# Gated delta rule on one Trainium2 core: shared solve tiles, compact state, and a new order of outputs and scores

## The reference

```python
lower = where(tri_strict, einsum(k_beta, k) * decay, 0)
sol = triangular_solve(I + lower, [v_beta, k_beta * exp(g)])       # u, w
attn_intra = einsum(q, k) * decay
def step(state, inp):
    v_new = u_i - w_i @ state
    o_i = q_i @ state + a_i @ v_new                    # q_i carries exp(g)
    state = state * gl + k_i^T @ v_new                 # k_i carries exp(g_last - g)
```

## Time and profile before

| what | value |
|---|---|
| median of 3 runs (lowest, highest) | 2690.39 us (2690.27, 2694.24) |
| span of the profiled execution | 2685.3 us |
| busy, PE / PEld / DVE / ACT / POOL | 96% / 77% / 68% / 34% / 20% |
| mean granted TensorE clock | 0.985 |
| the changed loop | from about 397 to 603 us |

### The profile page before, as it was taken

The page is one execution under the profiler, slowest core; times in us unless marked ns, Lnnn a source line. Parts: engine busy times, 40 slices in busy tenths (PEclk is TensorE's granted clock), DMA queues, the critical chain, the costliest instruction groups (busy, mean ns, idle before and its releaser), DMA issues. The chain is left out here.

```text
span 2685.3 us, 35832 instructions
## 1 busy us (share of the span) xinstructions
PE 2583.9 (96%) x14026; PEld 2060.8 (77%) x14026; DVE 1817.1 (68%) x2735; ACT 926.3 (34%) x1610; POOL 549.2 (20%) x265
## 2 busy tenths in 40 slices
PE   7999999999899999999999999999999999999998
PEld 5875558884478887788888888867997888887787
DVE  5894997772667668999773553333277666666987
ACT  4335454420444545333332222232233223232432
POOL 1212544430000004333201222134400000003330
PEclk9999999999999999999999999999999999999999
DMA  4011032230133336333221222243413222225231
GB/s 162 32 64 67 32 126 96 90 133 24 55 114 118 103 118 223 111 110 126 91 82 53 78 70 75 81 166 108 145 55 88 79 87 79 87 79 214 100 126 63
DMA packets 192759, 262.24 MB, mean 98 GB/s; under 512 B 15952, under 2 KB 121808, under 8 KB 192208
## 3 DMA queue, kind: packets, MB, share of 16 engines
q1 hardware_dynamic: 192592, 259.95, 28.6%
HBM read 196.80 MB, written 61.93 MB: 96 GB/s over the span
## 5 line engine op out<-in xcount | busy, mean ns | idle before, releaser
L1381 PE MATMUL ps<-gl_t,gl_slot 128*128 128x512 f32 x1056 | 244.6, 391 | 2.4 <-DVE gl_t L3986 2.4
L1389 PE MATMUL ps<-b_hi,a_hi 128*128 128x512 f32 x592 | 231.6, 391 | 9.5 <-DVE sb L3630 7.6
L1381 PEld LDWEIGHTS ps<-gl_t,gl_slot 128*128 128x128 f32 x1056 | 199.3, 189 | 44.6 <-DVE gl_t L3986 3.1
L2756 POOL TENSOR_TENSOR s_raw<-ff_raw 128x1024 f32<-128x1024 f32 x2 | 5.1, 2545 | 962.6 <-DMA ff_raw<-hid_rows 513.6
L3630 DVE TENSOR_TENSOR sb<-sb,ps 128x512 f32<-128x512 f32 x272 | 173.5, 680 | 33.3 <-PE ps L1389 33.2
L1381 PE MATMUL ps<-gl_b,gl_slot 128*128 128x512 f32 x768 | 182.1, 395 | 3.7 <-DVE gl_slot L4018 3.7
L1381 PE MATMUL ps<-ff_t,slot 128*128 128x512 f32 x768 | 179.2, 393 | 4.4 <-DVE ff_t L3284 4.4
L1381 PE MATMUL ps<-H_hi,tw_hi 128*128 128x512 f32 x448 | 175.6, 392 | 0.0
L1381 PE MATMUL ps<-H_rest,tw_hi 128*128 128x512 f32 x448 | 174.4, 389 | 0.0
L1381 PE MATMUL ps<-H_hi,tw_lo 128*128 128x512 f32 x448 | 174.3, 389 | 0.0
L1381 PEld LDWEIGHTS ps<-gl_b,gl_slot 128*128 128x128 f32 x768 | 146.4, 191 | 35.1 <-DVE gl_slot L4018 2.4
(11 more groups left out here) (475 smaller groups left out, 6053.9 us busy)
## 6 DMA issues: line engine op xcount, KB each, us to landing
wraw<-in_w_ff SPq DMA_DIRECT2D x16, 1024.0 KB, 5.9
ff_raw<-ff_rows SPq DMA_DIRECT2D x8, 2048.0 KB, 7.9
slab_raw<-in_w_ff SPq DMA_DIRECT2D x16, 1024.0 KB, 5.1
ff_rows<-quad SPq DMA_DIRECT2D x61, 256.0 KB, 2.0
traw<-in_w_in SPq DMA_DIRECT2D x28, 512.0 KB, 4.3
wq_raw<-in_w_in SPq DMA_DIRECT2D x6, 2048.0 KB, 8.5
wraw<-in_w_gate SPq DMA_DIRECT2D x22, 512.0 KB, 3.9
wraw<-in_w_up SPq DMA_DIRECT2D x22, 512.0 KB, 5.1
```

The lines of the kernel that those rows point to most:

```text
L1381: mm = nc.tensor.matmul(out_ap, stationary(a, k), moving(c, k), start=(k == 0 and n == 0), stop=(k == kts - 1 and n == 2))
L1389: mm = nc.tensor.matmul(out_ap, stationary(a, k), moving(c, k), start=(fresh and k == 0 and n == 0), stop=(k == 1 and n == 2), skip_group_ ...
L2756: G.tensor_tensor(s1, s3, a22, ALU.add).then_inc(dn_as, 1)
```

## The change

Each line is what the code does.

- The values and the rest of the solve share tiles: `X_of(i, c)` is in `KVt[i % 2][c]`. Tile 0 holds direction 0's rows 0 to 63 and direction 1's rows 64 to 127, the halves both solve first; tile 1 holds the others. `kv_load` fills them with six transfers a step instead of two. `Xw` and its first copies on GpSimd are gone.
- One `forward` and one `less_forward` of 128 rows serve both directions. Forwards 1 and 2 write 64 rows a direction from 128; forward 3 writes 32 from 32. Heads alternate between the directions.
- The state `Sc` is compact (4x64 columns a direction, no zero blocks, no memset). `update` and `carried` go head by head.
- The decay on the carried keys is multiplied into `KdT` by GpSimd ahead, instead of scaling the product by `ECUM` on VectorE; `less_carried` is one subtraction per tile and half.
- "kk" and "kq" become one matmul of 256 columns a head ("sc"), in four parts a step, two a direction. The weights share a tile (`weights`), and GpSimd's `decay_args` waits for all four of a direction.
- Order: direction 0's outputs of the step before and its scores stay between the stages; the last own output of direction 1 and both parts of its scores stand behind the update, ahead of the carried term.
- The loads of `w_out` are cut: the first half's rows 0 to 3 wait for the last solve, and the residual's second half for the outputs of step 6.

```diff
-        Gm = [[area(AT_X + 4096 + 2048 * b + 1024 * d, HEADS, P) for d in range(2)] for b in range(2)]
-        ATm = [[area(AT_H + 2048 * b + 1024 * d, HEADS, P) for d in range(2)] for b in range(2)]
+        weights = [[area(at_g + 2048 * d, HEADS, 2, P) for d in range(2)] for at_g in (AT_X + 4096, AT_H)]
+        KQ = area(AT_WORK + 12288, 2, 4 * SEQ).rearrange("p n (q c) -> p n q c", c=SEQ)
         KVt = [[area(AT_W + 2048 * b + 1024 * d, 2 * GW) for d in range(2)] for b in range(2)]
+        KV_LOADS = 16 * 6
+        def X_of(i, c):
+            return KVt[i % 2][c][:, GW:2 * GW]
-        Xw = [area(AT_W + 6144 + 512 * d, GW) for d in range(2)]
-        Sbd = [[area(gd + 1024 * b + 512 * d, 4, P) for d in range(2)] for b in range(2)]
+        Sc = [[area(gd + 512 * b + 256 * d, 4, HD) for d in range(2)] for b in range(2)]
+        KdT = [area(gd + 1024 + 512 * d, 4, P) for d in range(2)]
...
+        def mixed_rows_of(i, c):
+            return tile_of(c, i), tile_of(1 - c, i)
...
             def kv_load(i):
                 if i >= 2:
-                    sp.wait_ge(gdn_X, 2 * (i - 1))
+                    solved(sp, i - 2)
                     sp.wait_ge(gdn_kd, 2 * (i - 1))
-                for d in range(2):
-                    sp.dma_start(KVt[i % 2][d], kv_rows[tile_of(d, i)]).then_inc(kv_in[i % 2], 16)
+                for c in range(2):
+                    dst = KVt[i % 2][c]
+                    sp.dma_start(dst[:, 0:GW], kv_rows[tile_of(c, i)][:, 0:GW]).then_inc(kv_in[i % 2], 16)
+                    for x, t in enumerate(mixed_rows_of(i, c)):
+                        part = slice(HD * x, HD * x + HD)
+                        sp.dma_start(dst[part, GW:2 * GW], kv_rows[t][part, GW:2 * GW]).then_inc(kv_in[i % 2], 16)
...
+            solved(sp, NT - 2)
+            wov_0, wov_1 = (w_out[:, 512 * h:512 * h + 512].rearrange("(k p) n -> p k n", p=P) for h in range(2))
+            sp.dma_start(wout_late, wov_0[:, 4:8]).then_inc(slab_in[0], 16)
+            sp.dma_start(wout_1, wov_1).then_inc(slab_in[1], 16)
             sp.wait_ge(gdn_rexp, 2 * NT)
             sp.wait_ge(gdn_arg, 2 * NT)
             for h in range(2):
                 if h == 1:
-                    for d in range(2):
-                        wait_full(sp, G_GDN, GDN_AT[("w", NT - 1, d, 3)])
+                    for p in range(4):
+                        wait_full(sp, G_GDN, GDN_AT[("o", NT - 2, p)])
                 sp.dma_start(X[:, 4 * h:4 * h + 4, :], xv[:, 4 * h:4 * h + 4, :]).then_inc(xin_in, 16)
+            solved(sp, NT - 1)
+            sp.dma_start(wout_early, wov_0[:, 0:4]).then_inc(wout_in, 16)
...
+            def scores(i, d, part):
+                if i >= NT:
+                    return
+                banks = [bank("sc", i, d, part, x) for x in both]
+                t = tile_of(d, i)
+                for j in both:
+                    for x in both:
+                        q = 2 * part + j
+                        keys_and_queries = KQ[HD * x:HD * x + HD, :, q, t * P:(t + 1) * P]
+                        mm = nc.tensor.matmul(heads_of(ps[:, banks[x], 256 * j:256 * j + 256], P), tokens(KTall, 2 * q + x, d, i),
+                                              keys_and_queries, start=True, stop=True)
+                        if j == 1:
+                            mm.then_inc(full[banks[x]], 1)
...
+            def carried(i, c):
+                for d in both:
+                    ready("kv", i - 1, d)
+                    pe.wait_ge(gdn_keys, 2 * (i - 1) + d + 1)
+                banks = [bank("kS", i, c, x) for x in both]
                 for q in range(4):
-                    mm = nc.tensor.matmul(ps[:, b, q * P:(q + 1) * P], pair_tile(KTall, q, d, i), Sbd[d][i % 2][:, q, :],
-                                          start=True, stop=True)
-                mm.then_inc(full[b], 1)
+                    for x in both:
+                        for r in both:
+                            d = c if r == 0 else 1 - c
+                            part = slice(HD * r, HD * r + HD)
+                            mm = nc.tensor.matmul(ps[part, banks[x], q * HD:(q + 1) * HD], half(KdT[d], 2 * q + x)[:, part],
+                                                  half(Sc[d][i % 2], 2 * q + x), start=True, stop=True)
+                        if q == 3:
+                            mm.then_inc(full[banks[x]], 1)
...
+            def forward(i, s):
+                for d in both:
+                    if s == 1:
+                        weights_ready(pe, i, d)
+                    ready("y", i, d, s - 1)
+                b = bank("w", i, s)
                 for h in range(HEADS):
-                    mm = nc.tensor.matmul(ps[rows, b, h * HD:(h + 1) * HD], Gm[i % 2][d][:, h, rows],
-                                          yv[i % 2][d][:, h * HD:(h + 1) * HD], start=True, stop=True)
+                    for d in both:
+                        rows = block_rows(d, 3) if s == 3 else slice(HD, P) if (s == 2) != (d == 1) else slice(0, HD)
+                        seen = block_rows(d, 2) if s == 3 else slice(0, P)
+                        mm = nc.tensor.matmul(ps[rows, b, h * HD:(h + 1) * HD], weights[i % 2][d][seen, h, 0, rows],
+                                              yv[i % 2][d][seen, h * HD:(h + 1) * HD], start=True, stop=True)
                 mm.then_inc(full[b], 1)
             def update(i, d):
@@ -1625,73 +1689,86 @@
                 ready("y", i, d, 3)
                 b = bank("kv", i, d)
                 for q in range(4):
-                    cols = slice(q * P, (q + 1) * P)
-                    mm = nc.tensor.matmul(ps[:, b, cols], Kdec[d][:, cols], yv[i % 2][d][:, cols], start=True, stop=True)
+                    for x in both:
+                        cols = slice((2 * q + x) * HD, (2 * q + x + 1) * HD)
+                        mm = nc.tensor.matmul(ps[x * HD:(x + 1) * HD, b, q * HD:(q + 1) * HD], Kdec[d][:, cols],
+                                              yv[i % 2][d][:, cols], start=True, stop=True)
                 mm.then_inc(full[b], 1)
-            def outputs(i, *parts):
-                for p in parts if i >= 0 else ():
-                    d = p // 2
-                    pe.wait_ge(gdn_qd, 2 * i + d + 1)
-                    ready("y", i, d, 3)
-                    for x in range(2):
-                        ready("kq", i, d, x)
-                    b = bank("o", i, p)
-                    for q in (2 * (p % 2), 2 * (p % 2) + 1):
-                        if i > 0:
-                            nc.tensor.matmul(ps[:, b, q * P:(q + 1) * P], QdT[(i + 2) % 3][d][:, q, :], Sbd[d][i % 2][:, q, :],
-                                             start=True, stop=False)
-                        for h in (2 * q, 2 * q + 1):
-                            cols = slice(h * HD, (h + 1) * HD)
-                            mm = nc.tensor.matmul(ps[:, b, cols], ATm[i % 2][d][:, h, :], yv[i % 2][d][:, cols],
-                                                  start=(i == 0), stop=(i == 0 or h % 2 == 1))
-                    mm.then_inc(full[b], 1)
...
             for i in range(NT):
                 more = i + 1 < NT
                 if i > 0:
-                    for d in both:
-                        carried(i, d)
-                outputs(i - 1, 0, 1)
+                    for c in both:
+                        carried(i, c)
                 solve(i, 0)
                 if i == 0:
                     for d in both:
-                        scores("kq", 0, d)
-                outputs(i - 1, 2)
-                for d in both:
-                    forward(i, d, 1)
-                outputs(i - 1, 3)
+                        first_scores("kq", d)
+                else:
+                    carried_outputs(i - 1, 0)
+                forward(i, 1)
+                if i > 0:
+                    own_outputs(i - 1, 0, 0)
                 solve(i, 1)
-                if more:
-                    scores("kk", i + 1, 0)
-                for d in both:
-                    forward(i, d, 2)
-                if more:
-                    scores("kq", i + 1, 0)
+                if i > 0:
+                    own_outputs(i - 1, 0, 1)
+                forward(i, 2)
+                scores(i + 1, 0, 0)
                 solve(i, 2)
-                if more:
-                    scores("kk", i + 1, 1)
-                for d in both:
-                    forward(i, d, 3)
-                if more:
-                    scores("kq", i + 1, 1)
+                scores(i + 1, 0, 1)
+                if not more:
+                    carried_outputs(i, 0)
+                forward(i, 3)
+                if i > 0:
+                    carried_outputs(i - 1, 1)
+                    own_outputs(i - 1, 1, 0)
                 solve(i, 3)
                 if more:
                     for d in both:
                         update(i, d)
-            outputs(NT - 1, 0, 1, 2, 3)
+                if i > 0:
+                    own_outputs(i - 1, 1, 1)
```

(149 more changed lines are left out.)

133 lines of the change are left out of this document (61 added, 72 removed).

## The result

The changed kernel takes 2751.86 us (2749.97 to 2753.36, 4 runs) against 2690.33 before: a ratio of 1.0227, interval 1.0213 to 1.0242. The forecast was 2694 with a range to 2712.

A forecast was written before the change was run, and what follows sets the result against it. It took a serial zigzag of four solves, beside a slower mask loop, to bound the loop. Terms -0.7 - 1.6 - 3.5 + 4.5 - 0.35 - 1.0 + 6.4 gave +3.7 us on 2690.39: 2694, range 2684 to 2712.

The forecast's parts named there:

- Shared tiles and one subtraction: Three forward stages of a step: one subtraction of 0.68 us, 0.72 less a stage; forwards one and two 1.1, third 1.08.
- The rival that column halves don't overlap: Forwards one and two and the update run longer: 2.5 us a step, 15 over six, 2709; chance 0.22.
- The prediction's sign against itself: First and second forward at 1.8 us or more for 32 records would show the forecast wrong.
- Update, carried term, moved work: Behind the last solve: update 1.1 us, own outputs 0.95, scores part 1.05, carried term 2.2; first solve starts at 6.8.
- The new wait: First copy stands behind ScalarE's exponentials: forward one 11.5 us behind the update, 2.3 longer; TensorE idle 2.6 us.
- The stall of the state's decay: VectorE's decay of the state beside GpSimd's four multiplications: 0.45 us a step charged, between 0 and 1.5.
- The clock: TensorE's new wait comes six times; four followed by half clock at 1.6 us: +6.4, between 0 and 18.
- six gaps at 3: Upper bound of the clock term: all six new waits of TensorE cost 3 us each, 18 us.
- Sum: All terms over loop start, steps, last step, tail and clock: +3.7 us on 2690.39, prediction 2694.
- clock falls at every gap and stays: Rival for TensorE's clock at the new waits: 6 x 3 = 18 us instead of 6.4, 2706; chance 0.14.

The follow-up runs named there:

- a6_apart: a1_copy_first with the forward's two loops exchanged, so one direction's records come first instead of alternating; 2706.48 us, ratio 1.0061.
- a2_fill: Changed kernel, wait kept, with two idle products of 128x512 ahead of forward one of steps 1 to 6, inside the wait; 2688.87 us, ratio 1.0008.
- a7_dense_later: Changed kernel, wait kept unfilled, with two idle products of 128x512 ahead of forward three of steps 1 to 6; 2745.11 us, ratio 1.0207.
- a1_copy_first: Changed kernel with direction 1's exponentials moved behind the second copy of the next step on ScalarE, instead of ahead of its first; 2692.93 us, ratio 1.0021.

## Why the prediction was wrong, point by point

**Shared tiles and one subtraction: right.** One subtraction of 0.68 to 0.69 a stage; forwards 1.15 (taken as 1.1) and third forward 1.08. The rival that column halves don't overlap fell: a6_apart shows it as an experiment. The Trainium skill, "TensorEngine Tiling (Array Packing)", section Tiling Modes, says that column tiles over all rows load and multiply independently; these runs agree where the records alternate (1.15 us) and not where they don't (1.87), which the trace of before could not show. The prediction's sign against itself, a forward of 1.8 us or more, would have misled: forward one does take 1.98 us, but by the clock, and 1.15 at full clock.

**Update, carried term, moved work: right within 0.2 us but for one term.** Update 1.15 (1.1), own outputs 1.10 (0.95), a part of the scores 1.00 (1.05), carried outputs 1.11 (1.0). The carried term was put at 2.2 us and took 1.20, since four blocks of 64x64 overlap; it changed nothing, as VectorE's weightings end last there.

**The new wait: right.** Forward one at 11.86 (11.5), idle 2.61 (2.6), once a step, released by ScalarE; in the steps behind this one the idle time is 3.15 to 3.31.

**The stall of the state's decay: right at full clock,** 0.40 to 1.35 us in a2_fill by where it meets GpSimd. In the changed kernel itself the two never meet, and it takes 0.40 to 0.42 each time.

**The clock: this step failed.** The text took four falls at 1.6 us, +6.4, between 0 and 18, with prices from two early waits of the old loop. The direction was right, and nearly the place: every one of steps 2 to 6 loses its clock at the wait. The size was off by ten: 2751.86 - 2688.87, with and without the filling, is 63 us. The failed term is the price of one fall. Steps 2 to 6 take 33.3 to 38.3 us, against 25.1 to 25.9 in a2_fill: 8 to 13 us a fall instead of 1.6, and no step is spared. The two prices had been read where half clock lasted 3.5 us (405.3 to 408.8) and 7 us (425.8 to 432.8); in the changed loop it lasts 14 to 34. The bound "six gaps at 3" kept those lengths. Even the old loop had a warning that was not read as one: in its tail the clock stayed at half for 10 us through outputs that left no gap, until the wide products of `w_out` had begun. In the changed kernel that tail is at half clock from 647.6 to 668, again until within the wide products.

**Sum.** Without the clock term the text gives 2694.1 - 6.4 = 2687.7; a2_fill measured 2688.87. The agreement is partly luck, for a2_fill does not take only that term away: half clock is left in its steps 0 and 1 (406 to 423 and 433 to 443). In its profiled execution the five steps behind update 1 take 128.0 us (forecast 127.7), but from the first solve to update 0 it takes 22.6 (19.0, which the changed kernel met) and from there to update 1 29.1 (25.2), while the last step takes 21.3 (22.1) and the tail 7.8 (10.0). Its loop ends 3.2 us later than before, where the forecast without the clock has 2.7 us earlier.

The rival "clock falls at every gap and stays", with a chance of 0.14, had the number of falls nearly right (each of steps 1 to 6, and two more at updates) and priced them at 3 us each, 2706 instead of 2752; the range was cut off by the same bound. The prediction also cites the earlier trace rows for the last chain; that row shows only the span, and nothing in the sum hangs on it.

What stays open: which property of the new step keeps the clock down and lets it fall at the update. The forward's alternation is not needed for the fall (a6_apart; whether it helps to keep the clock down was not taken apart). It is not idleness alone (19.78 of 20 us busy), and wide products shorten it (a7_dense_later); narrower scores, the compact state, the order or the joint effect were not taken apart. Nor do the runs say why small products alone brought the clock back after 14 us in some steps and after 31 to 34 in others.

## What to carry to other kernels

A wait on TensorE in a loop of small products has two prices: its length, and the clock afterwards. The second can be several times what a fall cost in another loop (8 to 13 us a step here, against prices of 1.0 and 2.2 read before); read from the rows what TensorE did when the clock last rose, not only when it fell. Before adding work behind a loop's critical product, follow every tile that it frees late to the in-order queue where its refill stands ahead of something urgent: here a reordering by one place in ScalarE's list, and a useless product in the last gap, turned +2.3% into -0.7%.

## What the runs showed of the hardware that was not expected

- Half clock persisted while TensorE was occupied 99% of the time (460 to 480 in the changed kernel), with fp32 products of 32 to 128 rows and 64 to 256 columns. Such products brought it back too, 14 to 34 us behind the fall; a pair of fp32 products 128x128 by 512 columns did it within the pair or at its end (four steps of a7_dense_later, three of a2_fill).
- The clock also fell with no gap longer than 0.71 us directly ahead: at 517.6 and 589.5 in the changed kernel, at 544.3 in a1_copy_first. The kernel before has a gap of 0.68 at the same place in every step and is at 1.00 from 440 to 520.
- Two such products in a gap, whose results nobody reads, made the kernel 63 us faster; one made it 20 us faster. The Trainium skill, "TensorE: Matmul & The Clock Gate", section HAM oscillation, tells of a loop that loses its clock at every wait. The changed kernel agrees for the waits, with a fall at each of steps 2 to 6 and 0.50 to 0.76 of full clock in the windows from 480 to 600.
- Blocks of 64x64 that alternate over all four quarters of the array ran 64 records in 1.20 us, 0.019 a record, against 0.036 for two column halves (1.15/32).
